# Eight-core encoder block: a mask moved to TensorE, a filter tap moved to VectorE, one matmul of 129 columns, more loads in flight

## What is computed

```python
x = x + 0.5 * swiglu(rmsnorm(x, norm_ffn1), w_ffn1_in, w_ffn1_out)
h = rmsnorm(x, norm_mix)
aq, ak, av, mq, mk, mv, mo, mif, cq, gts = split(h @ w_in)
# attention: 24 heads of 64; 8 heads for each (window w, dilation r) of (128,1), (512,4), (2048,16)
#   keys of the same residue class mod r with |i - j| <= 64 in that class; masked scores are -1e30
#   out = sum over the three groups, weighted by their softmax denominators
# mLSTM: 4 heads of 128, chunks of 128, forward and backward
mqk = silu(centred_dwconv(concat(mq, mk), ml_conv_w, ml_conv_b))   # 5 taps for each channel
C_new = decay * C + sum_s wk_s * v_s k_s^T                         # state, 128 x 128
n_new = decay * n + sum_s wk_s * k_s                               # its normaliser, 128
# merge
x = x + (sum_b sigmoid(gate_b(h)) * (branch_b @ W_b)) @ w_out
x = x + 0.5 * swiglu(rmsnorm(x, norm_ffn2), w_ffn2_in, w_ffn2_out)
out = rmsnorm(x, norm_final)
```

## Time and profile before

| | us |
|---|---|
| median of 3 runs | 3931.39 (3927.96 to 3935.42) |
| the profiled execution's own time | 3924.01 |
| its span on the slowest core | 3922.5 |
| spans of the 8 cores | 3913.1 to 3922.5 |
| TensorE busy in the span | 3789.1 |
| VectorE, ScalarE, GpSimd busy | 1843.3, 1450.1, 1049.0 |

### The profile page before, as it was taken

How to read it: one execution, slowest core, us unless ns; L and a number is a source line. 1 busy time by engine, 2 the same in 40 slices (tenths; PEclk the granted TensorE clock), 3 DMA queues, 4 the chain that set the end, 5 groups by cost and what they waited for, 6 DMA issues and landing times.

```text
span 3922.5 us, 64917 instructions; the slowest of 8 cores (3913.1 to 3922.5 us)
## 1 busy us (share of the span) xinstructions
PE 3789.1 (97%) x23896; PEld 1914.7 (49%) x23896; DVE 1843.3 (47%) x2644; ACT 1450.1 (37%) x2401; POOL 1049.0 (27%) x1049
## 2 busy tenths in 40 slices
PE   7999999999989999999989999999999899999998
PEld 3444466644554444444434444666455544444444
DVE  3121446668884444121542214466688744532215
ACT  4101244477775222101331013444777742321012
POOL 2010224346770012000321002234476611110002
PEclk9999999999999999999999999999999999999999
DMA  6152332433434333222433214225243434332212
GB/s 138 24 83 32 88 68 47 93 88 65 72 82 95 69 78 46 37 42 37 117 103 61 38 23 115 44 58 111 62 79 60 97 75 76 67 52 39 38 23 90
DMA packets 254629, 265.74 MB, mean 68 GB/s; under 512 B 161648, under 2 KB 181360, under 8 KB 252016
## 3 DMA queue, kind: packets, MB, share of 16 engines
q0 software_dynamic: 65232, 127.00, 21.7%
q1 hardware_dynamic: 189088, 134.58, 12.3%
HBM read 318.25 MB, written 57.67 MB: 96 GB/s over the span
## 4 chain that ended last, share of the span: by engine, by line
PE 89%; DVE 4%; issue 2%; ACT 2%; DMA 1%; POOL 1%; SPq 0%; DVEq 0%; POOLq 0%; ACTq 0%
PE ps L467 89%; DVE arena L467 4%; ACT arena L467 2%; POOL arena L467 1%; DMA arena<-x 0%; DMA arena<-w1a 0%; DMA arena<-scr_v 0%; ACT L467 0%; SPq L467 0%; DVEq L466 0%; ACTq L466 0%; POOLq L484 0%; POOLq L466 0%; DVEq L484 0%; SPq L466 0%
## 5 line engine op out<-in xcount | busy, mean ns | idle before, releaser
L467 PE MATMUL ps<-arena 128*128 128x512 bf16 (+6 forms) x23896 | 3789.1, 319 | 124.3 <-DVE arena L467 75.6
L467 PEld LDWEIGHTS ps<-arena 128*128 128x128 bf16 x23896 | 1914.7, 99 | 1998.5 <-issue 248.2
L467 ACT ACTIVATE arena<-ps 128x512 bf16<-128x512 f32 (+6 forms) x1347 | 815.9, 638 | 1694.4 <-PE ps L467 1668.7
L467 DVE TENSOR_TENSOR arena<-ps,arena 128x512 f32<-128x512 f32 (+4 forms) x936 | 736.3, 799 | 1422.2 <-PE ps L467 1351.8
L467 POOL TENSOR_TENSOR arena<-arena 128x512 f32<-128x512 bf16 (+4 forms) x592 | 805.6, 1376 | 764.8 <-ACT arena L467 359.4
L467 ACT ACTIVATE arena<-arena 128x512 f32<-128x512 f32 (+5 forms) x719 | 429.9, 614 | 342.1 <-DVE arena L467 303.6
L467 DVE SCALAR_TENSOR_TENSOR arena<-ps,arena 128x512 f32<-128x512 f32 (+3 forms) x496 | 343.6, 700 | 373.7 <-PE ps L467 349.9
L467 DVE TENSOR_TENSOR arena<-arena 128x512 bf16<-128x512 f32 (+4 forms) x432 | 372.3, 873 | 51.7 <-ACT arena L467 12.0
L467 ACT ACTIVATE arena<-ps,arena 128x512 f32<-128x512 f32 (+2 forms) x256 | 160.5, 647 | 347.9 <-PE ps L467 343.2
L467 DVE SCALAR_TENSOR_TENSOR arena<-arena 128x512 bf16<-128x512 f32 (+3 forms) x304 | 229.9, 820 | 43.6 <-ACT arena L467 37.3
L467 POOL DMA_DIRECT2D arena<-wst x120 | 68.2, 568 | 517.9 <-PE ps L467 512.1
(11 more groups left out here) (16 smaller groups left out, 33.6 us busy)
## 6 DMA issues: line engine op xcount, KB each, us to landing
arena<-wst POOLq DMA_DIRECT2D x120, 256.0 KB, 4.4
arena<-w1a POOLq DMA_DIRECT2D x88, 256.0 KB, 5.0
arena<-w2a POOLq DMA_DIRECT2D x88, 256.0 KB, 4.6
arena<-x SPq DMA_DIRECT2D x32, 512.0 KB, 6.7
scr_x<-arena SPq DMA_DIRECT2D x8, 2048.0 KB, 11.0
arena<-scr_x SPq DMA_DIRECT2D x32, 512.0 KB, 9.1
out<-arena SPq DMA_DIRECT2D x28, 512.0 KB, 4.2
scr_v<-arena SPq DMA_DIRECT2D x48, 256.0 KB, 2.9
```

The source lines that it names most:

```text
L467: ins = getattr(eng, rec.name)(**rec.kwargs)
```

## The change

Six edits:

1. The mask of `td` is applied as in `tc_`: the last 2048 columns of `amask` hold 0 and -30000 instead of 1 and 0, and `add` becomes true for `moff >= 1024`. For 64 units (4 windows, 2 heads, 4 pairs, 2 sequences) the VectorE multiplication goes and a matmul of 512 columns comes.
2. In `conv` three taps are matmuls and two are VectorE instructions. The second of these reads the result of the first in on-chip memory. There are 64 convolution blocks (8 channel groups, 4 token blocks, 2 sequences). `dg` has three matrices.
3. `upair` issues one matmul of 129 columns for C and n.
4. At the end of a window `Ln` reads the bank with the stride and writes (i r), so that the multiplication on VectorE has one strided input (the bank) instead of two. Counts stay.
5. The first loads are chained by `xl[-5]`, and the first weights by `xl[0]` while the list is short.
6. Numbers of `_cost`: VectorE with two inputs on chip, and with two strided inputs of which one is in PSUM; GpSimd with long or strided inputs.

```diff
@@ _cost @@
             if len(tens) == 2 and not psum:
-                rec.cost = rec.cost * 1.1 + self.shared
+                rec.cost = rec.cost * 1.1 + self.shared * (1.7 if all16 else 0.9)
+            if psum and len(tens) == 2 and all(v.ap[-1][0] > 1 for v in tens):
+                rec.cost += 360.0
...
+            if self.shared and len(tens) == 2 and nin >= 512:
+                rec.cost += 150.0
             if any(v.ap[-1][0] > 1 for v in tens):
-                rec.cost += 500.0
+                rec.cost += 430.0
@@ host_consts @@
-        m2.append(np.tile((np.abs(A - bq) <= 64).astype(np.float32), (1, 16)))
+        m2.append(np.tile(np.where(np.abs(A - bq) <= 64, 0.0, NEGM).astype(np.float32), (1, 16)))
@@ load_x @@
-                                after=xl[-3] if paced and len(xl) > 3 else None))
+                                after=xl[-5] if paced and len(xl) > 5 else None))
@@ ffn, first weights @@
-                        xl.append(S.dma(out=wb[:, 0], in_=wa_d[i], queue="pool", after=xl[-3]))
-                        xl.append(S.dma(out=wb[:, 1], in_=wa_d[22 + i], queue="pool", after=xl[-3]))
+                        xl.append(S.dma(out=wb[:, 0], in_=wa_d[i], queue="pool", after=xl[-5] if len(xl) > 5 else xl[0]))
+                        xl.append(S.dma(out=wb[:, 1], in_=wa_d[22 + i], queue="pool", after=xl[-5] if len(xl) > 5 else xl[0]))
@@ core_steps, qk @@
-                    add = moff == 1024
+                    add = moff >= 1024
@@ core_steps, pv @@
-                        S.act.activation(out=r1[a0:a0 + 64, :], in_=ps[d0:d0 + 64, bk, :], func=AF.Ln)
+                        S.act.activation(out=r1[a0:a0 + 64, :].rearrange("p (i r) -> p i r", r=4),
+                                         in_=ps[d0:d0 + 64, bk, :].rearrange("p (r i) -> p i r", r=4), func=AF.Ln)
...
-                                            in1=r1[a0:a0 + 64, :].rearrange("p (r i) -> p i r", r=4), op=ALU.mult)
+                                            in1=r1[a0:a0 + 64, :].rearrange("p (i r) -> p i r", r=4), op=ALU.mult)
@@ stage1, conv @@
-                        for j in range(4):
+                        for j in range(3):
                             S.pe.matmul(out=bank(bk), lhsT=dg[:, j, :], rhs=cb[:, tb * 512 + j:tb * 512 + j + 512],
-                                        start=(j == 0), stop=(j == 4 - 1))
+                                        start=(j == 0), stop=(j == 3 - 1))
                         src = bank(bk)
-                        for j in range(4, 5):
+                        for j in range(3, 5):
                             cs = cvr.next()
@@ stage2, upair @@
-                        S.pe.matmul(out=ps[:, bk, d_ * 256:d_ * 256 + 128], lhsT=ktok[:, c, :], rhs=vd[d_][:, c, 0:128],
-                                    start=True, stop=True)
-                        S.pe.matmul(out=ps[:, bk, d_ * 256 + 128:d_ * 256 + 129], lhsT=ktok[:, c, :], rhs=vd[d_][:, c, 128:129],
+                        S.pe.matmul(out=ps[:, bk, d_ * 256:d_ * 256 + 129], lhsT=ktok[:, c, :], rhs=vd[d_][:, c, 0:129],
                                     start=True, stop=True)
```

More of the change, by code:

```diff
@@ L1439, in mlstm_branch @@
                                  vd=[nn(BF16, [16, 130]) for _ in range(2)], gs=nn(BF16, [16, 128])))
-            dgr = Rot([nzz(BF16, [4, 128]) for _ in range(3)])
+            dgr = Rot([nzz(BF16, [3, 128]) for _ in range(3)])
             wmv = Rot([nzz(BF16, [8, 256]) for _ in range(2)])
@@ L1497, in proj @@
                             dg = dgr.next()
-                            S.pool.tensor_tensor(out=dg, in0=ident_f.unsqueeze(1).to_broadcast([128, 4, 128]),
-                                                 in1=vcol(V_CW + ch * 5, 4).unsqueeze(2).to_broadcast([128, 4, 128]), op=ALU.mult)
+                            S.pool.tensor_tensor(out=dg, in0=ident_f.unsqueeze(1).to_broadcast([128, 3, 128]),
+                                                 in1=vcol(V_CW + ch * 5, 3).unsqueeze(2).to_broadcast([128, 3, 128]), op=ALU.mult)
                             w = wq.next()
```

## The result

The changed kernel takes 3916.0 us (median of its executions) against 3931.4 before. The ratio is 0.9965, with a 95% interval of 0.9951 to 0.9979, so it is faster by 14 us (8 to 19). The forecast was 3899, 32 us faster. The sign was right and the wide range (3870 to 3922) held the result, but the forecast's own range (3885 to 3912) did not, and the size was less than half of what was forecast. The profiled execution took 3920.3 us, its span 3918.7. Ratios and profiles leave out the executions in which the cores of a die ran at a lower granted clock, and where too few were left for an interval the table gives the fastest in us.

What follows compares the result with a forecast made beforehand. TensorE bounds the kernel everywhere but the attention core, where VectorE is late. From 3924.0 us, -6.0 - 13.8 + 13.8 - 24 - 2 = -32 gave 3892, or 3899 as median; own range 3885 to 3912, wide range 3870 to 3922.

Steps and rivals of the forecast that it cites:

- -13.8: mLSTM stage: 64 convolution matmuls of 512 columns go from TensorE, 215.6 ns each, saving 13.8 us, all on the path.
- -6.0: mLSTM stage: 240 one-column matmuls go at 25 ns each, saving 6.0 us, all in the stage without gaps.
- TensorE hides them: mLSTM stage: 64 added VectorE taps of 0.8 us, 26 us a sequence, stay under TensorE's cover; price 0 to +10 us.
- the new cost numbers: Scheduler's model: they only move instructions; counted within the 55% cut of waits and given nothing of their own.
- the tap costs what it saves: Rival, mLSTM stage: second tap delays state chain and bank release, TensorE gaps of 10 us each sequence; 3919, chance 0.06.
- -24 of waits: Attention core: less VectorE work cuts TensorE's waits for it, -20 us in long stretches, -4 in short; bounds 0 and -47.5.
- +13.8 of matmuls: Attention core: 64 mask matmuls of 512 columns come on TensorE at 215.6 ns each, +13.8 us, at worst all added.
- the masks fall into the gaps: Rival, core: 40 of 47.5 us of waits go and half the mask matmuls are hidden; -58 us, 3873, chance 0.15.
- The strided `Ln`: Window end: strided `Ln` taken at 0 extra; multiplication falls 0 to 0.36 us, half taken, 4.3 us of VectorE in 249.
- the slower rival: Window ends: strided `Ln` costs ScalarE +0.36 us or more, 23 us on the chain; +15 us, 3946, chance 0.08.
- The loads: First 84 us: earlier first weight load and x blocks against a delayed norm; -6.4 to +3 us, -2 taken.
- The wait changes its owner: Rival, core: gaps stay since ScalarE and the single output bank set the pace; -14 us, 3917, chance 0.14.

Runs made afterwards that it cites:

- tap_only: The kernel before with the convolution tap alone moved from TensorE matmuls to VectorE (edit 2); ratio 1.0009, mLSTM stages 536.4 us.
- tap_and_costs: The kernel before with the moved convolution tap and the new cost numbers, nothing else; ratio 1.0011, mLSTM stages 536.5 us.
- mask_only: The kernel before with the mask of `td` on TensorE alone, old cost numbers; ratio 0.9965, cores 590.1 us against 607.7.
- loads_only: The kernel before with five weight loads in flight at first in place of three, nothing else; no ratio, fastest execution 3927.5 us.

## Why the prediction was wrong

The sum held three large parts, and the stages let each be checked.

**The step that failed is the convolution tap with the one-column matmuls in the mLSTM stage: -13.8 and -6.0, "all on the path", with "TensorE hides them" for the taps.** Forecast -19.8 us, measured +6.9 (536.1 to 543.0). I took the stage's 233.5 of 234 us of busy TensorE as proof that what leaves TensorE leaves the time. The runs show this in its place, in the mLSTM stages:

- The tap alone brought nothing: 536.4 us (`tap_only`) and 536.5 (`tap_and_costs`), against 533.2 to 537.5 with the queues of before. With the matmuls simply left out 5.3 us came back, of 13.8, with later work moved in; with the taps simply added the stages were 4.8 us longer. These two are not clear of their own orders.
- The duration of the taps was forecast nearly right (0.8 against 0.86 to 0.92 us). Wrong was that VectorE at 59% has room for them at no price: TensorE's waits for VectorE from 505 to 700 us went from 0.4 to 5.1 us, and the timeline shows a tap in front of state updates.
- The 240 one-column matmuls bring some 2 to 3 us, not 6.0: 2.2 by the means without the tap, 3.1 (536.4 to 533.3) in the one pair with the order held.
- The order that the model writes when both are there costs 9.1 us (533.3 to 542.4), 6.3 in the changed kernel; to the core 4.2 and 2.5. I gave the new cost numbers nothing for the order they write, and did not consider that merging two matmuls changes the order as well.

By the means of the kernels with equal queues, the stages went from 535.3 us to 536.5 with the tap, to 534.9 with the merged matmul in the order held, and to 541.9 in the order of the changed kernel. These steps add up by their making; what they show is that nearly the whole loss came with the last one. Why this order is worse is not settled. The model's 57 ns is the truer count, by the starts of the earlier trace rows, so a truer number wrote a worse order.

The rival "the tap costs what it saves" named the right place and the size of the gaps: 10 us for each sequence (idle 5.9 to 16.5 and 7.0 to 16.5 us). But the tap alone makes only half of them (12.9 to 23.3 us for both sequences); the rest came with the merged matmul. That its time, 3919, is close to the 3916 measured is in part luck: in its sum the mLSTM stages were even and the core 10.2 us shorter, where 6.9 longer and 23.0 shorter were measured. I gave it 0.06 because TensorE waited only 0.5 us there before. That small number told how well the order covered the chains, not how much slack they had.

**The core came out better than forecast.** -24 of waits and +13.8 of matmuls made -10.2 in the sum; measured -23.0 (607.7 to 584.7). By the runs this is -17.6 for the mask (`mask_only`), about -9 for edit 4 with the order held, and +3 to +4 for the new cost numbers (581.5 to 584.5 without the tap, 580.9 to 584.7 with it). The waits for VectorE fell by 19.9 us, near the 24. Too high was the price of the 64 mask matmuls. In `mask_only`, which has them and no other edit, TensorE's busy time is 3790.0 us, the median of the six cores whose records are complete, and before 3783.4: 6.6 us more with a matmul in flight, not 13.8 (`loads_only`, with TensorE's queue as before, reads 3786.2). The slowest core's page can't be used for this, since 428 of its 23960 matmul records are missing (one for each weight load is due). Part 1 of it:
```profile
PE 3765.9 (96%) x23532; PEld 1916.2 (49%) x23960; DVE 1781.0 (46%) x2580; ACT 1447.5 (37%) x2397; POOL 1046.5 (27%) x1049
```
They ran largely where the rows had shown TensorE waiting or with a matmul in flight: this much of the rival "the masks fall into the gaps" was right, though its 40 us of waits did not go. How the 17.6 us of this edit divide into shorter waits, filled ones and the new order is not separated further.

**The strided `Ln`** costs nothing (592 ns), and the multiplication lost all of its 0.36 us where I counted half: the slower rival had no ground, and the edit was worth more than I gave it. **The loads** had the wrong sign, by 3 to 4 us in all. **The new cost numbers** were a loss alone (1.0023), not nothing.

The two stages together are 16.1 us shorter and the total only 11.3: the rest of the program is 4.8 us longer. Of this 1.2 us are idle time in the first 100 us, where the loads are; the others are not explained.

**"The wait changes its owner"** landed at 3917, close to the time measured, by a mechanism that did not occur: TensorE's waits for VectorE in the core did shrink. The agreement with its time says nothing for it.

## What to carry to other kernels

A busy share near 100% on one engine, in a stage where its queue is fed by chains through other engines, is no proof that a saved instruction saves its time: take the instruction away with nothing in its place, and separately add its replacement. Where a model writes the order, any edit of an instruction's cost is an edit of the order too; hold the order fixed (count the new instruction as the old ones) to see what the edit itself is worth, and then look at orders for themselves. Even then compare several kernels with the same queues before you trust a few microseconds of a stage, and look at what work stands inside its edges. Of the changed kernel's edits the mask was worth the most (17.6 us of core), then the single stride (9 us); a better order for the same instructions was worth another 13.

## What the runs showed of the hardware

- VectorE's multiply-add of 512 columns with both inputs in on-chip memory (the second tap) takes 0.74 us in one place and 1.57 us in another of the same stage. On one core of the changed kernel 48 of the 64 take 0.74 to 0.76 us and 16 take 0.89 to 1.65; at each of the 16 a GpSimd instruction was in flight, mostly a 128x516 multiplication, and at 12 of the 48 as well. The first tap, with one input in PSUM, takes 0.73 to 0.75 us in all 64, 33 of them beside GpSimd. So a long one went with GpSimd at work and two inputs on chip, as in the rule of the Trainium skill that the prediction weighed (SBUF — State Buffer, section "Who interferes with whom"). Its price here was 3.6 to 5.4 us of VectorE in a sequence.
- A VectorE multiplication of 64 x 512 with a stride on both inputs takes 1041 ns, with a stride on the PSUM input alone 685. ScalarE reading the same bank with the stride takes 592 ns, as without (591).
- A matmul's time in flight is counted as busy (one-column matmuls: 61 ns each in the group, 25 ns from start to start), so the order alone moves the busy time. The changed kernel, in two runs, and the fastest one issue the same 23656 matmuls; over the cores with complete records their median busy times are 3780.9 and 3775.1 against 3767.7 us. One core proves little here, since cores of one run differ by up to 16.4 us (3772.0 to 3788.5). So "idle" and "busy" are soft measures of an order, and the lengths of stages are the safer ones.
